# Multiplying rows of zero weight into an open accumulation on TensorE

## The reference, cut to what matters

```python
def block(xb):                       # 128 tokens
    qh = einsum('td,de->te', xb, w_q)
    ...                              # scores, two top-16, one top-16 of the sums: eidx, g
    act = gelu(einsum('td,thkd->thk', xb, u_tab[eidx]))
    return einsum('thk,thkd->td', (g * act), v_tab[eidx])
```

## Time and profile before

| | |
|---|---|
| median of 3 runs | 4186.25 us |
| the profiled execution, its own time | 4192.47 us |
| its span, first to last instruction | 4190.7 us |
| mean granted TensorE clock | 0.740 |
| TensorE matmuls busy | 71% |
| VectorE, ScalarE, GpSimd busy | 60%, 25%, 54% |
| HBM traffic over the span | 330 GB/s |

### The profile page before, as it was taken

How to read it: one execution, slowest core, us unless ns; L and a number is a source line. 1 busy time by engine, 2 the same in 40 slices (tenths; PEclk the granted TensorE clock), 3 DMA queues, 4 the chain that set the end, 5 groups by cost and what they waited for, 6 DMA issues and landing times. The chain is left out here.

```text
span 4190.7 us, 51549 instructions
## 1 busy us (share of the span) xinstructions
PE 2957.0 (71%) x18028; PEld 1592.9 (38%) x18028; DVE 2498.7 (60%) x6770; ACT 1055.9 (25%) x2882; POOL 2263.1 (54%) x2365
## 2 busy tenths in 40 slices
PE   7989997777577758775877598759885665333364
PEld 6745554434244425432543254325542322000011
DVE  2445656766775676668666866686567546644400
ACT  3312212222322232223222322232322111111121
POOL 1102433665665566556565655565555656666665
PEclk9989998787587757885778578857686666555557
DMA  7635898999999999999999999999899999999998
GB/s 207 183 122 181 267 337 277 370 376 360 356 361 351 349 370 351 345 353 365 327 361 359 369 315 351 348 368 314 308 379 335 374 343 357 357 374 366 372 365 321
DMA packets 568768, 1387.77 MB, mean 331 GB/s; under 512 B 57384, under 2 KB 252384, under 8 KB 568512
## 3 DMA queue, kind: packets, MB, share of 16 engines
q0 software_dynamic: 335024, 1215.35, 77.8%
q1 hardware_dynamic: 221264, 159.49, 12.2%
q10 hardware_dynamic: 12224, 9.63, 0.8%
HBM read 1353.19 MB, written 30.95 MB: 330 GB/s over the span
## 5 line engine op out<-in xcount | busy, mean ns | idle before, releaser
L1870 DVE CUSTOM_DVE_ANT_0 d_ub<-d_ub,d_pX 128x1024 f32<-128x1024 f32 x1024 | 1240.3, 1216 | 635.2 <-DMA d_ub<-in_peer_u_dram,d_eid 540.3
L1657 POOL DMA_INDIRECT d_ub<-in_peer_u_dram,d_eid x1152 | 1121.3, 973 | 904.3 <-DVE d_hdot L1870 419.3
L1676 POOL DMA_INDIRECT d_vb<-in_peer_v_dram,d_eidT x1096 | 1059.0, 966 | 883.0 <-PE d_pY L1706 441.6
L1706 PE MATMUL d_pY<-d_vb,d_dg 128*32 128x256 f32 x8768 | 930.9, 516 | 781.6 <-DMA d_vb<-in_peer_v_dram,d_eidT 545.9
L1706 PEld LDWEIGHTS d_pY<-d_vb,d_dg 128*32 128x32 f32 x8768 | 257.7, 129 | 1353.2 <-issue 1145.1
L1745 ACT ACTIVATE d_dg<-c_late_sb,d_wgtT 128x32 f32<-128x32 f32 x1152 | 338.4, 315 | 1357.3 <-PE d_pY L1706 823.0
L695 PE MATMUL d_pX<-d_wq,d_vb 128*128 128x512 f32 (+3 forms) x1536 | 469.6, 458 | 15.4 <-DMA d_vb<-in_w_in_dram 8.6
L695 PEld LDWEIGHTS d_pX<-d_wq,d_vb 128*128 128x128 f32 x1536 | 267.9, 198 | 181.1 <-issue 111.7
L847 PE MATMUL d_pS<-t_mdg,t_E 128*128 128x128 f32 x1152 | 205.4, 338 | 42.5 <-ACT t_AT L970 21.9
L847 PEld LDWEIGHTS d_pS<-t_mdg,t_E 128*128 128x128 f32 x1152 | 181.2, 241 | 109.7 <-issue 68.3
L832 PE MATMUL d_pS<-t_shared 32*128 32x512 f32 (+3 forms) x384 | 183.4, 668 | 39.2 <-issue 20.0
(11 more groups left out here) (275 smaller groups left out, 3562.7 us busy)
## 6 DMA issues: line engine op xcount, KB each, us to landing
d_vb<-in_w_in_dram SPq DMA_DIRECT2D x68, 512.0 KB
d_ub<-in_peer_u_dram,d_eid POOLq DMA_INDIRECT x1152
d_vb<-in_peer_v_dram,d_eidT POOLq DMA_INDIRECT x1096
r_side<-in_cache_k_dram SPq DMA_DIRECT2D x16, 1024.0 KB
r_side<-in_cache_v_dram SPq DMA_DIRECT2D x16, 1024.0 KB
d_wo<-in_w_out_dram SPq DMA_DIRECT2D x6, 2048.0 KB, 8.1
d_wo<-in_peer_w_q_dram SPq DMA_DIRECT2D x4, 2048.0 KB, 10.7
scratch_h<-t_shared SPq DMA_DIRECT2D x9, 512.0 KB
```

The source lines that it names most:

```text
L1657: pool.indirect_dma_start(out=ub[:, g % R, :], out_offset=None, in_=io["peer_u"][0], in_offset=off).then_inc(u_in[g % R], 16)
L1676: pool.indirect_dma_start(out=to, out_offset=None, in_=io["peer_v"][0], in_offset=off).then_inc(landed, 16)
L1706: m = nc.tensor.matmul(pY[q * QT:(q + 1) * QT, g % 2, :], dg[:, n % DG, :], rows[:, q * QD:(q + 1) * QD], start=k % QT == 0, stop=k % QT = ...
L1870: nc.vector.tensor_tensor_reduce(out=ub[:, g % R, :], in0=ub[:, g % R, :], in1=xflat if i else xn_of(0), scale=1.0, scalar=0.0, op0=ALU.mu ...
```

## The change

In periods 1 to 6 (`1 <= i < NT - 2`), in steps k below 88 that don't open a sum (`k % 32` not 0), TensorE first issues four more matmuls: weights are the 31 zero columns of `hot`, the moving operand is 256 columns of `keysT`, and the result is added to 31 of the 32 rows of each quarter of the open half of `pY`. They wait for nothing and signal nothing. There are 85 such steps in a period, 510 in all. The computed values stay as they were.

```diff
+                def keep_on(k):
+                    none = hot[:, QT:2 * QT - 1]
+                    for q in range(4):
+                        nc.tensor.matmul(pY[q * QT:(q + 1) * QT - 1, k // QT % 2, :], none, keysT[:, 0:2, :], start=False, stop=False)
+
...
                             if k == 0:
                                 turn_weights(i - 1)
+                            if k % QT and k < 88 and 1 <= i < NT - 2:
+                                keep_on(k)
                             weigh_rows(i - 1, k)
```

## The result

The changed kernel takes 4209.58 us (median of 18 runs, 4188.37 to 4242.65); the kernel before, measured beside it, takes 4173.42 us (18 runs, 4156.43 to 4196.23; the 4186.25 us of the prediction were the median of three of them). The ratio is 1.0087, 95% interval 1.0069 to 1.0104: 36 us slower. The profiled execution took 4212.93 us, with a span of 4211.2 us and a mean granted clock of 0.786 (before 0.740).

What follows compares the result with a forecast made beforehand. The prediction took the gathers as the bound, TensorE second. Fillers' 274 us less 125 us saved by the clock left 149 us more busy time, of which 32 us reach the end: 4186 + 32 = 4218 us, range 4140 to 4290 us.

Steps and rivals of the forecast that it cites:

- reading (a): Six stretches, steps 0 to 87 of periods 1 to 6: 0.7% of time per busy-share point, 64 us; half taken, 32.
- Price of a filler: TensorE's time for one more filler next to others: 0.43 us at 2.4 GHz, 0.845 us at 1.2 GHz.
- Clock 0.87: Granted clock in steps 0 to 87 of periods 1 to 6, lifted by the fillers from 0.78 by 0.09.
- bound from periods 8 and 9: Upper bound on the clock's lift in periods 1 to 6: doubled row density is worth 0.16, from 0.50 to 0.66.
- Net busy time +149 us: TensorE, steps 0 to 87 of periods 1 to 6: fillers cost 274 us, the higher clock saves 125 us.
- (b): Same six stretches: the half clock is what hurts the gathers, so fillers that raise the clock are free.
- There a filler costs nothing: Where TensorE waits for v rows, a filler is free: 211 us in 115 places, 59 us for nothing shown.
- Waits for landings below 120 us: TensorE's waits for v rows in the six stretches should fall from 211 us to below 120 us.
- Traffic 340 to 350 GB/s: Gather traffic expected in the six stretches; above 355 GB/s with busy share past 88% would prove the prediction wrong.
- the faster one: In periods 1 to 6 the clock holds at 0.94 or more, rows leave sooner: 40 us gained, 4146 us; chance 0.27.
- No change: In periods 1 to 6 fillers fall into waits or the clock pays for them: 4186 us; chance 0.21.
- The much slower one: In periods 1 to 6 zero-weight fillers don't lift the clock: 313 us more busy time, 4318 us; chance 0.10.

Runs made afterwards that it cites:

- kernel 4: Fillers only in periods 7, 8 and 9 (372), none in periods 1 to 6; ratio to the kernel before 1.0048, on chip A.
- kernel 2: The changed kernel with two fillers in front of each row in place of one; ratio to the kernel before 1.0207, on chip A.
- kernel 8: The changed kernel with 31 columns of key data as the fillers' weights in place of zeros; ratio to the kernel before 1.0035, on chip B.
- kernel 9: The changed kernel with fillers of 16 columns in place of 256, in the same 510 places; ratio to the kernel before 1.0072, on chip C.
- number 7: The changed kernel with the filler behind the row of v instead of in front; ratio to the kernel before 1.0064, on chip B.

## Why the prediction was right or wrong

The forecast was 32 us slower, measured are 36 us (4218 us forecast and 4209.58 measured, as the kernel before came out 13 us lower with more executions). The terms for TensorE's busy time and clock held. That half of reading (a) met the loss is largely luck, as told below. Step by step:

- **Price of a filler, 0.43 us at the full clock:** right for the filler that was forecast. It was taken from whole rows of v, with their eight matmuls and eight weight loads. For two fillers the same arithmetic gives a little too little: the clock of 0.955 leaves 9% of the time at the half level, so 1020 x (0.91 x 0.43 + 0.09 x 0.845) = 477 us are spent and 0.35 x 1715 x 0.83 x 0.49 = 244 us saved, net 233 us, where 261 to 288 were measured. As a rate per column, as the experiments took it, it fails: the kernels with 16 and 128 columns show a piece that doesn't shrink with them (about 0.2 us of the 0.43, an estimate).
- **Clock 0.87:** 0.88 to 0.89. The bound from periods 8 and 9 (0.16) held for the sum, but the same work density that gives 0.66 in period 9 gave 0.83 in period 8 of kernel 4, so the bound was lucky.
- **Net busy time +149 us:** 1534 and 1553 against 1417 and 1390, on average +140 us.
- **Half of reading (a), 32 us:** right in the sum, and luck in its reason. It was the middle between a reading of 64 us and one of nothing. Taken alone (b), that fillers which raise the clock are free, is contradicted by the loss, and (a), that the loss follows the busy share, by the kernels with 16 and 256 columns: busy time went up by 91 us and the clock by 0.07, and the time stayed. At 32 rows of the array busy time went up by 448 us with no lift, and half of that reached the end.
- **"There a filler costs nothing":** wrong on chip A, by 20 us for 372 fillers, most of them in waits (kernel 4). This is the step of the reasoning that failed, though the sum held.
- **Waits for landings below 120 us:** 158 us, and 173 us in the second profile of the changed kernel; the kernel before has 211 and 192 us. TensorE's lateness didn't use them up; why isn't shown.
- **Traffic 340 to 350 GB/s:** 331 to 367, mean 351. The first two stretches kept 365 and 367 GB/s at a busy share of 88%; had all six done so, the prediction named it as a sign against itself. This needn't be the clock's doing: kernel 4, with no filler there and a clock of 0.77, ran the same two stretches at 370 and 369 GB/s.
- **Rivals:** the faster one priced a clock of 0.94 at -40 us; kernel 2 reached 0.96 and lost 86 us. The clock held, but only by more work. No change held for the scores alone on chip B and for steps 1 to 15 on chip C. The much slower one fell with kernel 8 and with the clock of the changed kernel itself.

What stays open: what the waits "for issue" are. The traffic of TensorE's instructions grows with the fillers; the page's line of that queue for the kernel before on chip C, and for kernel 9 on the same chip (packets, MB, share of the 16 DMA engines):

```profile
q8 instruction: 147, 2.41, 0.2%
```

```profile
q8 instruction: 179, 2.93, 0.3%
```

That is 32 packets of 16 KB for 8160 instructions. These packets go through DMA engines that are 91 to 100% busy in the six stretches, so a late one is a conceivable reason for a wait for issue. Against it: in period 8 of kernel 4 the 85 waits are spread evenly over the 24 us between two such packets, and no kernel was run that changes the instructions' path alone. It is argued, not shown.

## What to carry to other kernels

Work added only to keep TensorE's clock up must be costed three times: its array time, the piece that doesn't shrink with its columns (here 16 instructions per filler; 510 of them lost some 30 us on chip C even with 16 columns), and the clock that it gives back. Here the clock gave back less than the fillers took, 117 to 163 us of busy time stayed, and cutting the columns didn't help. Put such work, if anywhere, where the clock is low (the scores cost nothing measurable, the projections 15 us) and give it the full height of the array. First ask whether the transfers leave anything to win: here, with a DMA share of 0.93 to 1.00, even 15 fillers that lifted the clock by 0.2 won nothing.

## What the runs showed of the hardware

- Busy time alone didn't lift the granted clock: the same 4080 matmul instructions gave 0.88 to 0.89 with 128 rows of the array and 0.73 with 32 (TensorE 96% busy), against 0.77 to 0.79 without them (81 to 83% busy); with 16 columns it was 0.81, with 128 columns 0.84.
- Zero weights lifted it as data did (0.88 to 0.89 and 0.88).
- Chips differ. On chip B the kernel before takes 3992 us, 4.4 to 5.0% less than on A and C, at nearly the same clock (0.75 against 0.74). Its transfers are faster: the 88 steps of period 8 take 228 us at 407 GB/s there, and 246 to 252 us at 366 to 369 GB/s on A and C in the kernels without fillers in it. GpSimd waits more for VectorE there than for TensorE (621 and 381 us in kernel 8), on C less (404 and 477 us in the changed kernel). On B TensorE hardly ever waits for issue: 20 us in 6 to 8 places in each of the four kernels, all of which have fillers, against 302 us in 241 places in the kernel before on C. The waits of the v row there (kernel 8) are for data and for VectorE; the kernel before on C, which has 146 us in 121 places for issue beside it, follows:

```profile
PE d_pY L1706 <- DMA d_vb<-in_peer_v_dram,d_eidT: 613.9, 436, 5.0
PE d_pY L1706 <- DVE d_xs L1845: 48.0, 18, 6.1
```

```profile
PE d_pY L1706 <- DMA d_vb<-in_peer_v_dram,d_eidT: 518.5, 290, 5.7
```

  The Trainium skill ("Runtime: NRT & Kernel Launch", "Instruction fetch mechanics") states that the loading of instructions is mostly hidden. Chip B agrees with it; on A and C the 173 to 425 waits for issue in each kernel speak against it, if that is what they are. On B the fillers cost 0.35% with data (number 8) and 0.64% behind the row (number 7) without such waits, so the loss doesn't need them. Fillers of few columns weren't run on B, and a ratio to the third digit holds for the chip that it was measured on.
